# Diagonal grams placed among the gate projections, and one retention gate projection between the two corner products of the inverse

## What is computed

```python
def hybrid_layer(x, ...):                      # twice
    h = rms_norm(x, norm_g) * (1 + scale) + shift
    proj = h @ w_in                            # pool_u, pool_g, q, k, v, ret_g, rw, rw_g, gate_logits
    o_pool = causal_pool_mixer(pool_u, pool_w, pool_scale) * silu(pool_g)
    o_ret  = retention(q, k, v, positions, ret_norm_g) * silu(ret_g)
    o_rwkv = rwkv7_time_mix(rw, ...) * silu(rw_g)
    y = einsum('btnw,nwd->btnd', [o_pool, o_ret, o_rwkv], w_branch)
    return x + gate * (sum(sigmoid(gate_logits) * y) @ w_out)
```

## Time and profile before

| | before |
|---|---|
| runs, median (lowest to highest) | 1835.14 us (1833.32 to 1837.72) |
| profiled execution: own time, span | 1840.28 us, 1838.2 us |
| TensorE matmul busy | 1718.2 us, 93% |
| VectorE, ScalarE, GpSimd busy | 1036.0 (56%), 800.7 (44%), 632.0 (34%) |
| mean granted TensorE clock | 0.968 of full speed |
| weight split, ScalarE (L1041), GpSimd (L1525), mean of one | 1.06 us, 2.47 us |
| Silus of pg0 and pg1, one projection apart | 158.31 and 163.75 us |

### The profile page before, as it was taken

How to read it: one execution, slowest core, us unless ns; L and a number is a source line. 1 busy time by engine, 2 the same in 40 slices (tenths; PEclk the granted TensorE clock), 3 DMA queues, 4 the chain that set the end, 5 groups by cost and what they waited for, 6 DMA issues and landing times. The chain is left out here.

```text
span 1838.2 us, 26011 instructions
## 1 busy us (share of the span) xinstructions
PE 1718.2 (93%) x10688; PEld 1373.8 (75%) x10688; DVE 1036.0 (56%) x1367; ACT 800.7 (44%) x1200; POOL 632.0 (34%) x344
## 2 busy tenths in 40 slices
PE   8999989999999899899999999989999999987783
PEld 6877778888888787688888888868888986544441
DVE  4346744666665325584556766443116627866675
ACT  2455522333223335542333222344337736866673
POOL 1336612424444434751243444433421021322210
PEclk7999989999999899998999999989999999999997
DMA  8223321215444323322122544333420067999994
GB/s 344 81 92 106 90 77 36 92 58 192 171 166 171 126 92 96 96 85 77 54 85 66 209 175 169 138 126 126 149 92 1 1 240 265 382 388 395 389 392 178
DMA packets 82605, 287.97 MB, mean 157 GB/s; under 512 B 30473, under 2 KB 30601, under 8 KB 65332
## 3 DMA queue, kind: packets, MB, share of 16 engines
q1 hardware_dynamic: 76708, 275.87, 41.6%
q0 software_dynamic: 5040, 8.25, 1.4%
q10 hardware_dynamic: 736, 2.14, 0.3%
HBM read 274.50 MB, written 22.61 MB: 162 GB/s over the span
## 5 line engine op out<-in xcount | busy, mean ns | idle before, releaser
L1525 POOL TENSOR_TENSOR wmem_r<-wmem,wmem_r 128x1024 fp32r<-128x1024 f32 x170 | 420.2, 2473 | 696.4 <-ACT wmem_r L1041 685.5
L721 PE MATMUL banks<-h_hi_r,wmem_r 128*128 128x512 f32 x1632 | 511.2, 392 | 6.9 <-POOL wmem_r L1525 6.9
L721 PEld LDWEIGHTS banks<-h_hi_r,wmem_r 128*128 128x128 f32 x1632 | 307.9, 189 | 77.0 <-POOL wmem_r L1525 9.4
L1041 ACT ACTIVATE wmem_r<-wmem 128x1024 fp32r<-128x1024 f32 x170 | 180.2, 1060 | 405.2 <-DMA wmem<-wstream 402.2
L721 PE MATMUL banks<-hT_r,wmem_r 128*128 128x512 f32 x816 | 319.0, 391 | 0.0
L721 PEld LDWEIGHTS banks<-hT_r,wmem_r 128*128 128x128 f32 x816 | 154.0, 189 | 31.3
L2725 DVE TENSOR_TENSOR slots_r<-slots,wmem_r 128x1024 fp32r<-128x1024 f32 x102 | 121.9, 1217 | 57.7 <-ACT wmem_r L2418 52.1
L2806 POOL TENSOR_TENSOR wmem_r<-wmem,wmem_r 128x1024 fp32r<-128x1024 f32 x30 | 74.8, 2493 | 202.3 <-ACT wmem_r L2276 202.3
L992 PE MATMUL banks<-slots_r,wmem_r 128*128 128x512 f32 x512 | 127.7, 389 | 0.0
L1465 DVE SCALAR_TENSOR_TENSOR ztp<-xT,c_act,ztp 128x256 f32<-128x256 f32 x168 | 122.8, 731 | 6.0
L741 PE MATMUL banks<-wmem_r,h_hi_r 128*128 128x512 f32 x384 | 118.9, 391 | 0.0
(11 more groups left out here) (450 smaller groups left out, 3043.1 us busy)
## 6 DMA issues: line engine op xcount, KB each, us to landing
wmem<-wstream SPq DMA_DIRECT2D x206, 512.0 KB, 3.3
slots<-experts SPq DMA_DIRECT2D x80, 1024.0 KB, 24.5
xT<-ada SPq DMA_DIRECT2D x24, 1024.0 KB, 5.8
xT<-experts SPq DMA_DIRECT2D x16, 1024.0 KB, 25.0
slots<-ada SPq DMA_DIRECT2D x8, 1024.0 KB, 18.0
x_keep<-xT SPq DMA_DIRECT2D x2, 2048.0 KB, 17.4
xT<-x_keep SPq DMA_DIRECT2D x2, 2048.0 KB, 8.1
dil_rows<-dil_once SPq DMA_DIRECT2D x1, 2560.0 KB
```

The costliest lines, as they stand in the source:

```text
L721: mm = nc.tensor.matmul(o, r(lhs[:, k, :]), r(rhs[:, k, :]), start=(k == 0 and i == 0), stop=(k == KD - 1 and i == 2))
L1041: inc(nc.scalar.activation(r(chunk(b)[0]), w, ACT.Copy), "w_high")
L1525: inc(g.tensor_tensor(r(lo), lo, r(hi), ALU.subtract), "w_split")
```

## The change

The job list and the programs of four engines are reordered; GpSimd's is not changed.

TensorE now does pg0, `dg`, pg1, `bs`, pg2, `tv` and `tb`, pg3, `tk`, `rg`, tg0 to tg2, `zp`, tg3, `zc`, `py`, `gram0` to `gram2`, scan. ScalarE takes the exponentials before the Silu of pg0, in the order end-of-step, prev, minus, plus; copies the grams out before the Silus of pg1 and pg2; takes pg3's between the `tb` and the `tk` copies; and copies `zp` out before tg3's Silu. VectorE forms KK and the first product of A behind all running sums and `g_prev`, instead of before the last quarter of the sums. SP loads the chunk behind pg1 between the two halves of the grams' stores, those behind pg2 to rg3 before the inverse's stores, and those behind tg0 and tg1 only after its spread.

```diff
         for c in range(CW):
             job(f"pg{c}", "pg_ready", 1 + c)
-        for c in range(CW):
-            job(f"bs{c}", "bonus_ready", 1 + c)
-        for x in range(NT // 2):
-            for e in range(2):
-                job(f"dg{x}{e}", "corner_ready", 1 + x)
+            if c == 0:
+                for x in range(NT // 2):
+                    for e in range(2):
+                        job(f"dg{x}{e}", "corner_ready", 1 + x)
+            if c == 1:
+                for i in range(CW):
+                    job(f"bs{i}", "bonus_ready", 1 + i)
+            if c == 2:
+                for n in range(NT):
+                    job(f"tv{n}", "tok_ready", 1 + n)
+                for n in range(NT):
+                    job(f"tb{n}", "tok_ready", NT + 2 * n + 2)
...
+            job(f"tk{n}", "tok_ready", 3 * NT + 2 * n + 2)
...
         for c in range(CW):
+            if c == CW - 1:
+                corner_jobs("zp", "p_ready")
             job(f"tg{c}", "retg_ready", 1 + c)
+        corner_jobs("zc", "z_ready")
...
-                          ("k_mod", 1), ("rk_ready", 1), ("kk_unit", 3), ("kn_stored", 16), ("kn_spread", 32), ("bonus_ready", 4),
+                          ("k_mod", 1), ("rk_ready", 1), ("kk_unit", 4), ("kn_stored", 16), ("kn_spread", 32), ("bonus_ready", 4),
@@ -641,15 +650,17 @@
-            load_chunks(FIRST["pu"] + 1, FIRST["rg"])
+            load_chunks(FIRST["pu"] + 1, FIRST["pg"] + 1)
             for n in range(0, NT, 2):
+                if n > 0:
+                    load_chunks(FIRST["pg"] + 1, FIRST["pg"] + 2)
                 after("dg_ready", n // 2 + 1)
                 for k in range(SUBS):
                     inc(sp.dma_start(dg_dram[k, n:n + 2].rearrange("n h i j -> i (n h) j"),
                                      dg_part[sub_rows(k), n:n + 2].rearrange("i n h j -> i (n h) j")), "dg_stored", 16)
             after("dg_stored", 8 * NT * SUBS)
             inc(sp.dma_start(wu_sb[:, :], dg_dram.rearrange("k n h i j -> (k n h) (i j)")), "dg_gathered", 16)
-            load_chunks(FIRST["rg"], FIRST["tg"] + 2)
+            load_chunks(FIRST["pg"] + 2, FIRST["tg"])
...
-            load_chunks(FIRST["tg"] + 2, FIRST["merge"] + 6)
+            load_chunks(FIRST["tg"], FIRST["merge"] + 6)
@@ -792,12 +803,7 @@
             project("pu")
-            project("pg")
-            after("rk_ready")
-            for c in range(CW):
-                o = open_bank(f"bs{c}")
-                full(nc.tensor.matmul(o, con("blk64"), X3[:, c, :], start=True, stop=True))
-
+            feature_job("pg0", FIRST["pg"])
             after("ar_ready", 1)
             after("bk_ready", 1)
...
+            feature_job("pg1", FIRST["pg"] + 1)
+            after("rk_ready")
+            for c in range(CW):
+                o = open_bank(f"bs{c}")
+                full(nc.tensor.matmul(o, con("blk64"), X3[:, c, :], start=True, stop=True))
+            feature_job("pg2", FIRST["pg"] + 2)
...
+            feature_job("pg3", FIRST["pg"] + 3)
...
-            project("rg")
-            project("tg")
-            pool_w = whole(FIRST["pool_w"])
-            for c in range(CW):
...
-            for m in range(GRAMS_FIRST):
-                gram(m)
+            project("rg")
+            for c in range(CW - 1):
+                feature_job(f"tg{c}", FIRST["tg"] + c)
             after("inv_spread")
             after("corner_ready")
             corner_products("zp", lambda at, i: zt[at, i, SUB:STEP], lambda at, i: tt[at, i, :], 1)
+            feature_job(f"tg{CW - 1}", FIRST["tg"] + CW - 1)
             corner_products("zc", lambda at, i: tt[at, i, :], lambda at, i: zt[at, i, SUB:STEP], 0)
+            pool_w = whole(FIRST["pool_w"])
+            for c in range(CW):
+                after("pool_d", c + 1)
+                o = open_bank(f"py{c}")
+                full(nc.tensor.matmul(o, pool_w[:, c * P:c * P + P], pool_u[:, c, :], start=True, stop=True))
+            after("ar_ready")
+
...
+            for m in range(GRAMS_FIRST):
+                gram(m)
             after("tok_ready")
             heads = [slice(c * RW_D, c * RW_D + RW_D) for c in range(CW)]
 
@@ -1079,20 +1094,23 @@
-            for c in range(CW):
+            if L == 0:
+                act.wait_ge(SEM["const_rest"], 16)
+            after("g_sum")
+            nc.scalar.activation(e_end[:, :, :], X2[:, :, STEP - 1:T:STEP], ACT.Exp, scale=DECAY)
+            after("g_prev")
+            inc(nc.scalar.activation(G_[:, :, :], G_[:, :, :], ACT.Exp, scale=DECAY, bias=con("off", 0)), "exp_prev")
+            after("kk_unit", 3)
+            inc(nc.scalar.activation(X1[:, :, :], X2[:, :, :], ACT.Exp, scale=-DECAY, bias=con("off", 1)), "exp_minus")
+            after("exp_minus")
+            inc(nc.scalar.activation(X2[:, :, :], X2[:, :, :], ACT.Exp, scale=DECAY, bias=con("off", 0)), "exp_plus")
+
+            def gate_out(c):
+
                 inc(nc.scalar.activation(pool_gate[:, c, :], bank(f"pg{c}"), ACT.Silu), "pg_ready")
                 high(FIRST["pg"] + c + RING)
-                if c == 1:
-
-                    if L == 0:
-                        act.wait_ge(SEM["const_rest"], 16)
-                    after("g_sum")
-                    nc.scalar.activation(e_end[:, :, :], X2[:, :, STEP - 1:T:STEP], ACT.Exp, scale=DECAY)
-                    inc(nc.scalar.activation(X1[:, :, :], X2[:, :, :], ACT.Exp, scale=-DECAY, bias=con("off", 1)), "exp_minus")
-                    after("g_prev")
-                    inc(nc.scalar.activation(G_[:, :, :], G_[:, :, :], ACT.Exp, scale=DECAY, bias=con("off", 0)), "exp_prev")
-                    after("exp_minus")
-                    inc(nc.scalar.activation(X2[:, :, :], X2[:, :, :], ACT.Exp, scale=DECAY, bias=con("off", 0)), "exp_plus")
+
+            gate_out(0)
...
                 inc(ins, "corner_ready")
+            gate_out(1)
+            gate_out(2)
             after("bk_ready")
             for n in range(NT):
                 inc(nc.scalar.activation(v_tok[:, n, :], bank(f"tv{n}"), ACT.Copy), "tok_ready")
             after("bonus_ready")
             for what, side in (("b", u_side), ("k", v_side)):
+                if what == "k":
+                    gate_out(3)
...
             after("pool_d")
+
+            def corners_out(name, dst, to, ready):
+
+                for x in range(NT // 2):
+                    after("bank_full", FULL[f"{name}{x}1"])
+                    for e in range(2):
+                        at = sub_of(e, to)
+                        o = bank(f"{name}{x}{e}")[at, :].rearrange("p (i t) -> p i t", t=SUB)
+                        inc(nc.scalar.activation(dst(at, slice(2 * RW_H * x, 2 * RW_H * (x + 1))), o, ACT.Copy), ready)
+
             for c in range(CW):
+                if c == CW - 1:
+                    corners_out("zp", lambda at, x: tt[at, x, :], 1, "p_ready")
                 inc(nc.scalar.activation(ret_gate[:, c, :], bank(f"tg{c}"), ACT.Silu), "retg_ready")
                 if c == 0:
                     high(FIRST["tg"] + RING)
...
+            corners_out("zc", lambda at, x: zt[at, x, SUB:STEP], 0, "z_ready")
@@ -1288,15 +1315,14 @@
 
             after("g_ready")
             for c in range(CW):
-                if c == CW - 1:
-                    after("kn_spread")
-                    step(v.tensor_tensor(KK[:, :, :], X1[:, :, :], KK[:, :, :], ALU.mult), "kk_unit")
-                    v.tensor_tensor(A_[:, :, :], A_[:, :, :], KK[:, :, :], ALU.mult)
                 for t0 in range(0, T, STEP):
                     last = v.tensor_tensor_scan(X2[:, c, t0:t0 + STEP], con("ones")[:, 0:STEP], G_[:, c, t0:t0 + STEP], 0.0,
                                                 ALU.mult, ALU.add)
             step(last, "g_sum")
             inc(v.tensor_tensor(G_[:, :, :], X2[:, :, :], G_[:, :, :], ALU.subtract), "g_prev")
+            after("kn_spread")
+            step(v.tensor_tensor(KK[:, :, :], X1[:, :, :], KK[:, :, :], ALU.mult), "kk_unit")
+            step(v.tensor_tensor(A_[:, :, :], A_[:, :, :], KK[:, :, :], ALU.mult), "kk_unit")
             after("exp_minus")
             inc(v.tensor_tensor(A_[:, :, :], A_[:, :, :], X1[:, :, :], ALU.mult), "bk_ready")
             after("exp_prev")
```

More of the change, by code:

```diff
@@ L324, in program, with corner_jobs @@
             job(f"pu{c}", "pu_ready", 1 + c)
+        def corner_jobs(name, ready):
+            for x in range(NT // 2):
+                for e in range(2):
+                    job(f"{name}{x}{e}", ready, 1 + 2 * x + e)
         for c in range(CW):
             job(f"pg{c}", "pg_ready", 1 + c)
-        for c in range(CW):
-            job(f"bs{c}", "bonus_ready", 1 + c)
-        for x in range(NT // 2):
-            for e in range(2):
-                job(f"dg{x}{e}", "corner_ready", 1 + x)
+            if c == 0:
[10 more added lines that the diff above has]
+                    job(f"tb{n}", "tok_ready", NT + 2 * n + 2)
         for n in range(NT):
[L333 to L336, removed]
```

(36 more changed lines are left out.)

## The result

The changed kernel takes 1848.18 us (median of 6 runs, 1843.98 to 1849.20), the kernel before in the same comparison 1836.33 (6 runs, 1833.32 to 1841.89). The ratio is 1.0064, 95% interval 1.0049 to 1.0078: slower, by 11.85 us. The forecast was 1840, 4.8 us more, with 1836 to 1846 as its own range and 1828 to 1849 as that of the whole prediction. The time lies in the second and outside the first: the sign was right, and the forecast had less than half of the size. The profiled executions took 1840.28 before and 1848.91 after, 8.63 apart; the one of before lay 4 us above its median, the other 0.7.

A forecast was written before the change was run, and what follows sets the result against it. TensorE, busy 93% of the span, was taken as the bound through its order, gaps and clock. Terms of +0.9 and +3.9 us per layer summed to +4.8: 1840 on the median; own range 1836 to 1846, whole range 1828 to 1849.

The forecast's parts named there:

- wait before the grams: TensorE before the diagonal grams, for VectorE's products: 4.9 and 4.3 us, with one GpSimd collision 6.1 in each layer.
- pg0 with its wait: First layer only: GpSimd's split of pg0 also meets the earlier KK product, +0.7 us; the wait before pg0 stays.
- low clock: grams and pg1: Behind the new gap: grams lose 2.0 us and pg1 2.1, taken as 4.1 a layer, ends 1.7 to 5.0.
- waits that go: Transpose waits, two shorter weight waits and the old corner-product waits go: 7.0 us in the first layer, 5.3 second.
- zp and zc: Corner and closing products, 256 records, begin at full clock: 2.7 and 2.4 us less, ends 0 and 3.3.
- first scan step: Scan entered at full clock: its first step falls to 5.0 us, 3.8 and 2.1 less, ends 0 and 4.
- wait at the corner products: Before the corner products: inverse's path ready 61.5 us after pg1's end, TensorE there at 60.9, so 0.6 us stays.
- wait at tg3: TensorE before tg3, whose load is issued behind the inverse's spread: new wait of 2.1 us, ends 0 and 5.
- low clock over tg3: The clock may fall behind the wait while tg3 runs: 0.8 us a layer, half of 1.7.
- A: Faster: scan-side gains hold, early grams are cheap, inverse and tg3's weights in time; 1825 in full, 1830 by half; chance 0.28.
- B: A stop before tg3 or in the corner products keeps the clock low; they and first scan step don't gain; 1851; chance 0.10.
- C: Sides cancel: wait 6 us, grams not slowed, wait at tg3 about 1; 1834, or up to 1837; chance 0.20.

The follow-up runs named there:

- two windows less: Changed kernel with GpSimd leaving out the window sums of pool blocks 2 and 3 (those pooled features not computed): 1828.15 us, ratio 0.9959 to the kernel before.
- SyncE's order: Changed kernel with the stores of A and KK ahead of pg1's load and tg3's load ahead of the inverse's stores: 1839.40 us, ratio 1.0017.
- back alone: Kernel before with only tg3 put between corner and closing products, pooling products and decay grams behind them: 1853.71 us, ratio 1.0113.
- the three edits together: Kernel before with the front part, the exponentials ahead of pg2's split, and pg1 ahead of the grams: 1828.76 us, ratio 0.9969.
- front part: Diagonal grams moved between pg0 and pg1, exponentials ahead of the Silus; alone against the kernel before: 1835.53 us, ratio 1.0010.
- back part: Tg3 put between corner and closing products, pooling products and decay grams behind them; alone against the kernel before: 1853.71 us, ratio 1.0113.
- The same edit: ScalarE's exponentials moved ahead of pg2's split: in the changed kernel 1843.67 us, ratio 1.0055; in the front part alone 1832.60 us, ratio 0.9974.

## Why the prediction had the sign and not the size

By its own steps, in us, first / second layer:

| step | predicted | measured |
|---|---|---|
| wait before the grams | +6.1 / +6.1 | +7.2 / +7.2 |
| pg0 with its wait | +0.7 / 0 | -1.9 / -2.6 |
| low clock: grams and pg1 | +4.1 / +4.1 | +1.2 / +1.3 |
| waits that go | -7.0 / -5.3 | -7.0 / -5.3 |
| zp and zc | -2.7 / -2.4 | -1.1 / -0.7 |
| first scan step | -3.8 / -2.1 | -3.5 / -1.8 |
| wait at the corner products | +0.6 / +0.6 | +5.9 / +4.2 |
| wait at tg3 | +2.1 / +2.1 | +1.0 / +1.8 |
| low clock over tg3 | +0.8 / +0.8 | +2.7 / +1.5 |
| sum | +0.9 / +3.9 | +4.5 / +5.6 |

The measured terms sum to 10.1 against 8.6 between the two executions. Most of the 1.5 between them is the transposes to token order, which the prediction had only by their waits: without these they took some 0.7 us less in each layer (`tv` 1.91 us instead of 2.36).

**Right.** The place and the releaser of the new wait, and its size within 1.1 us, that in part by luck. Of the difference between 6.1 and 7.2 us pg0's earlier end makes 1.6 in the first layer, and exp(-), ready at 159.0 and not 158.5, 0.5; the collision counted at 1.2 hardly came (products of 2.45 and 2.30): it hit the next two, of 4.45 and 4.49, which the grams don't need. The prediction's remark that the wait would be nearer 7 if both products were caught came true in its number and not in its way, since neither was. All removed waits went. The first scan step came to 5.28 and 5.27, forecast 5.0. The records of the corner products at full clock take 17.3 ns, forecast 16.4. The Trainium skill (TensorE: Matmul & The Clock Gate, "Wait — 56ns, not 53.3ns?") has a floor of about 25 ns; the trace doesn't agree, zc's 128 records took 2.21 us and not 3.2.

**The step that failed** is the wait at the corner products: the mechanism was there, as the last of the prediction's signs of being wrong ("the inverse reaching TensorE more than 3 us late") had it, and its size was off by 5.3 and 3.6. In the first layer: the inverse took 44.5 and not the 40.7 of the trace before (+3.8), TensorE came 59.9 and not 60.9 us after pg1's end (+1.0), the spread took 12.25 and not 11.3 (+0.9), and the inverse began 9.1 and not 9.5 us after pg1's end (-0.4): 0.6 + 5.3 = 5.9. In the second: +4.0, +1.0, -0.3, -1.1. So most of it is a duration that was carried over from the trace as if it belonged to the work. It belonged to what lay beside it, as the kernel with two windows less shows. The sign named in the prediction, that its DMAs wait on SP, was a part too: the pg1 load between the stores, taken with 9.5, can be put elsewhere for 2.1 us a layer.

**Its consequence** is the clock: a wait of 5.9 in place of 0.6 left zp at 3.63 us and most of tg3 at the low clock, 1.6 + 1.9 us more than forecast in the first layer. With no wait (two windows less) zp took 2.21 and tg3 5.7 us, and behind a wait of 1.3 (SyncE's order, first layer) zp took 2.21 and tg3 7.3. A third error had the other sign: pg0 ran at full clock behind a gap of 1.82 us where it had run at 0.77 behind 2.09, and pg1 had it too; 2.6 + 2.9 us less. Gaps of 2.1 to 2.8 us go either way in these traces: behind 2.09 and 2.79 (before) and 2.23 (back alone, second layer) the clock fell, behind 2.25 (the three edits together, second layer), 2.33 (two windows less, first layer) and 2.48 (back alone, first layer) it didn't, nor behind the 1.8 that most kernels with the front part have. The execution of before had caught the slow one twice; a gain that comes from the low stretches of one profile is counted against that profile and not against the median. The 3.2 us between 8.63 and 11.85 may be of that kind: the execution of before lay 3.95 above its median, the one after 0.73. In which gaps the other executions of before were quicker no trace shows.

**Rivals.** A (the inverse in time, tg3's weights too) falls for the changed kernel. With two windows less its condition was met behind the whole change, with waits before tg3 of 0.6 and 0.3 us, and the time, 1828.15, lay in A's 1825 to 1830, though the wait before the grams was 7.2 there and that kernel does less work. B's stop in the corner products took the clock down for zp and tg3, but not for zc and the scan, which had 2.21 and 5.28 us. C counted the grams as unslowed: they lost 1.2.

## What to carry to other kernels

Before work is taken from in front of a wait, measure the slack of the chain that the wait is for, and add to it what the chain will lose beside its new neighbours: a chain of short VectorE steps beside GpSimd has no fixed length. Here there was no slack before (a wait of 2.6 us), the front part brought the inverse's end 7 us forward, and the back part took 12 us of work from in front of the wait. The same edit is worth its full size or next to nothing depending on which wait comes next, so try it with and without the other part.

## What the runs showed of the hardware

- One two-input GpSimd instruction of 2.4 us stretches one 0.4 us VectorE step to 2.4 to 2.6, and no more than that one; the inverse's length went from 29.7 to 48.8 us over these kernels with the same 62 steps.
- Two splits beside VectorE's 128x2048 products took 8.81 us instead of 4.8, and the products 4.45 and 4.49 instead of 2.3: both sides lose.
- A standstill of 7.2 us was followed by only 3.4 us of work at the low clock, one of 5.9 by 10: in the first small tiles and then a projection ran, in the second small tiles, a stop of 1 us and then a projection. The length isn't fixed by the gap: behind the same 7.2 us the low clock lasted through the grams and a part of pg1 with SyncE's list reordered (grams 3.69 us, then 0.83 granted over the 6.8 us behind them). Why some recover sooner was not tested.
